# The last pair of down tiles of a mixture-of-experts layer: read as eight interleaved groups of sixteen rows in place of 128 adjacent rows

## The chip, the cores and the metric

One core of a Trainium2 chip runs the whole program. The metric is the device time of one execution in microseconds (us). The comparison is by the median of several executions; one execution was taken by the hardware profiler.

## What is computed

Two layers of a small network on 256 tokens of width 1024, in float32. The first has a recurrent mixer and a dense feed-forward block. The second has an mLSTM mixer and a mixture of eight experts, of which each token takes two. Only the end of the second matters here. Cut to that:

```python
def swiglu(x, w1, w3, w2):
    return (jax.nn.silu(x @ w1) * (x @ w3)) @ w2

def moe_swiglu(xn, w_router, w1, w3, w2):
    ...
    top_logit, top_idx = lax.top_k(logits, TOP_K)      # TOP_K = 2, N_EXPERTS = 8
    gates = jax.nn.softmax(top_logit, axis=-1)
    ...                                                # tokens gathered by expert
    yb = lax.map(expert_block, ...)                    # swiglu(xb, w1[e], w3[e], w2[e])
    ...
    out = jnp.zeros((T, D), xn.dtype).at[sorted_tok].add(y_slot)

x = x + moe_swiglu(rms_norm(x, norm_ffn), ...)
return rms_norm(x, final_norm)
```

w1 and w3 are [8, 1024, 2816], w2 is [8, 2816, 1024].

## The kernel before

The weights of the experts don't fit on the chip and pass through it once, in tiles of 128 partitions. The "up" weights (w1 and w3) come as 128 units of 1408 KB, from `moe13`, into ten slots. The "down" weights (w2) come as 88 pairs of 1024 KB, from `moe2`, into eight slots: `w2t`, four in the buffer W, three in S, and the eighth in x. A pair is 128 rows of 2048 float32, so 8 KB for each partition, and the 128 rows lie one behind the other in memory. There are NB = 11 pairs for each of E = 8 experts. Pair v is pair v mod 11 of the expert in place v // 11, and goes to slot v mod 8. Expert 7 in the order of places is the last; its pairs are v = 77 to 87. Pair 87, the last of all, goes to the slot in x.

All these transfers are issued by SyncE (SP) in one queue, in an order written out by hand: `first_refills` walks over the units and pairs in the order in which TensorE uses them. Before each it waits until TensorE has used the tile that stood in the same slot (`m_u` for units, `m_d` for pairs), and then issues the load of the tile that is ten units or eight pairs ahead. So pair 87 is issued when pair 79 is used. After it comes only the load of the weights of the final norm, `wrow`, 512 KB (4 KB for each partition, the same row for all). Which expert stands in which place is decided at run time; `chosen_rows` computes the address from a register.

Each load adds 16 to the semaphore of its slot. TensorE waits for it in `down` (the line before `w2p = ...`) and then runs 16 matmuls of 128x32 by 128x512 for the pair. In the last expert the pairs 0 to 10 run with nothing between them (`first_experts`), since all up units are done by then. Behind pair 87 come, in this order: ScalarE copies the result (L1644), TensorE scatters it to the tokens, VectorE adds it to the residual (L2325), ScalarE sums the squares (L1698), VectorE scales by the norm and by `wrow` (L2398), and SP writes the output (L649).

All matmuls of the kernel are recorded at one line, L692, the helper. The loads of pairs are L556, those of units L551, that of `wrow` L587.

Of the kernel before, what the change touches and what calls it, by code (L numbers as in the profile page):

```python
# [15 lines left out]
P = 128  # L16
T = 256
D = 1024
# [10 lines left out]
E = 8  # L29
# [9 lines left out]
NB = QN // 32  # L39
# [7 lines left out]
GATHERS = ((0, 1), (1, 4), (4, 8))  # L47
SMALL = (1, 4, 7)
SMALL_CAP = 64
ORDER = [7] + [SMALL.index(p) if p in SMALL else len(SMALL) + [q for q in range(1, E) if q not in SMALL].index(p) for p in range(1, E)]  # L50


# [20 lines left out]
def constants():  # L73

    s, t = np.arange(P)[:, None], np.arange(P)[None, :]
    c = np.zeros((P, NCONST), np.float32)
    c[:, IDENT:IDENT + P] = s == t
    c[:, BLK:BLK + P] = s // HD == t // HD
    c[:, ONES:ONES + P] = 1.0
    c[:, MEAN_D:MEAN_D + P] = 1.0 / D  # L80
    c[:, BLKM:BLKM + P] = (s // HD == t // HD) / HD
    c[:, SU:SU + P] = s < t
    c[:, FLOOR:FLOOR + P] = np.where(s <= t, 0.0, 1000.0)
    c[:, IOTA:IOTA + P] = t
    c[:, ROWS:ROWS + P] = np.concatenate([np.arange(32), np.arange(64, 96), np.arange(32, 64), np.arange(32, 64)])
    c[:, ROWS_LAST:ROWS_LAST + P] = np.concatenate([np.arange(32), np.arange(64, 96), np.arange(32), np.arange(64, 96)])
    c[:, RANKS:RANKS + E] = ORDER
    c[:, FIRST_KEY:FIRST_KEY + E] = [100000.0] + list(range(1, E))
    c[:, SHORT:SHORT + E] = [32.0 * (p in SMALL) for p in range(E)]
    c[:, CAPS:CAPS + E] = [SMALL_CAP if p in SMALL else SLOTS for p in range(E)]  # L90
    c[:, MEANS + 8] = 1.0 / D
    c[:, PICK:PICK + 32] = s % 32 == np.arange(32)[None, :]
    p = np.arange(P)
    c[:, TOK], c[:, TOK + 1] = p + 1, p + 1 + P
    c[:, QUARTER] = p // 32 - 4
    c[:, EVEN], c[:, ODD] = (p // 32) % 2 == 0, (p // 32) % 2 == 1
    c[:, EPS] = 1e-6
    c[:, EPS + 1] = 1e-5 * HD
    s, t = s % L, np.arange(L)[None, :]
    c[:, MASKS:MASKS + L] = s < t  # L100
    c[:, MASKS + L:MASKS + 2 * L] = s <= t
    c[:, EYE:EYE + L] = s == t
    low = np.zeros((P, LV, L), np.float32)
    for lv in range(LV):
        b = 1 << lv
        low[:, lv] = (s // (2 * b) == t // (2 * b)) & ((s // b) % 2 == 1) & ((t // b) % 2 == 0)
    c[:, LOW:LOW + (LV - 1) * L] = low[:, 1:].reshape(P, (LV - 1) * L)
    first = np.concatenate([(s // 2 == t // 2) & (s % 2 == 0) & (t % 2 == 1), low[:, 0] > 0], 1).astype(np.uint8)
    return c, first


def hybrid_rglru_rwkv7_mlstm_moe(nc, A, out):

    ctx = ExitStack()
    with ctx:
# [114 lines left out]
        u1, u2, u3 = [W[:, TMP + T * i:TMP + T * (i + 1)] for i in range(3)]  # L230
# [176 lines left out]
        def pair_slot(n, v):  # L407
            return v % (OVER_PAIRS if n else DSLOTS)
# [72 lines left out]
        def _(sp):  # L481
# [52 lines left out]
                sp.dma_start(m_all[:, h, :], m_rows[h:h + 1, :].broadcast_to([P, T])).then_inc(in_m, 16)  # L534
            u13 = A["moe13"].rearrange("(u p) n -> u p n", p=P)
            u2 = A["moe2"].rearrange("(u p) n -> u p n", p=P)

            expert = {}

# [4 lines left out]
            def chosen_rows(src, p, i, n):  # L544
                at = sp.snap(expert[p] * n + i, min_val=n, max_val=E * n - 1)
                return src[bass.ds(at, 1)].rearrange("u p n -> (u p) n")
# [5 lines left out]

            def load_d(n, v):
                p, i = divmod(v, NB)
                src = chosen_rows(u2, p, i, NB) if p else u2[v]
                sp.dma_start(w2t[pair_slot(n, v)], src).then_inc(in_d[pair_slot(n, v)], 16)  # L556

            def refill_unit(n, u):
# [9 lines left out]
            def refill_down(n, pair):  # L568
                ahead = OVER_PAIRS if n else DSLOTS
                if pair + ahead < PAIRED:  # L570
                    sp.wait_ge(m_d, PAIRED * n + pair + 1)
                    load_d(n, pair + ahead)

            def first_refills():
                for g in range(STAGES):
                    for k in range(KD):
                        refill_unit(0, g * KD + k)
                        if g * KD + k == KD + 2:
                            sp.wait_ge(ix_done, IX0 + 1)
                            load_d(0, 6)  # L580
                        for e, p in pairs_behind(g, k):
                            if NB * e + p + DSLOTS < NB * (E - 1):
                                refill_down(0, NB * e + p)
                for pair in range(NB * (E - 1) - DSLOTS, PAIRED - DSLOTS):
                    refill_down(0, pair)
                sp.wait_ge(m_u, LAST + 1)
                sp.dma_start(wrow, A["wf"].broadcast_to([P, D])).then_inc(in_wf, 16)  # L587
# [11 lines left out]

            load_u(0, 9)  # L600
            load_d(0, 3)
            sp.wait_ge(p1, 4)
            sp.dma_start(wo1, A["l1_w_out"].rearrange("(k p) n -> p k n", p=P)).then_inc(in_wo1, 16)
# [1818 lines left out]
def inputs_of(i):  # L2422

    def a(name):
        return np.asarray(i[name])
    o = {}
    o["xT"] = np.ascontiguousarray(a("x")[0].T)
    vecs = np.zeros((P, NV), np.float32)
    for name, at in VECS.items():
        if name == "moe_norm":  # L2430
            v = a("l1_norm_ffn").reshape(P, KD)
        else:
            v = a(name).reshape(-1, P).T
        vecs[:, at:at + v.shape[1]] = v
    o["vecs"] = vecs
    small = np.zeros((P, 4, 4, P), np.float32)
    for g, name in enumerate(("l0_gate_a_w", "l0_gate_x_w")):
        w = a(name).reshape(4, 2, HD, HD)
        for u in range(2):
            small[HD * u:HD * u + HD, g, :, HD * u:HD * u + HD] = w[:, u].transpose(1, 0, 2)  # L2440
    small[0:HD, 2] = a("l0_w_up").reshape(HD, 4, P)
    small[HD:, 2] = a("l0_a_up").reshape(HD, 4, P)
    small[:, 3] = a("l0_g_up").reshape(P, 4, P)
    o["small0"] = small.reshape(P, 2048)
    o["wqkv"] = np.ascontiguousarray(np.stack([a("l1_wq"), a("l1_wk"), a("l1_wv")]).transpose(2, 0, 1, 3)).reshape(P, 3 * D)
    wgt = np.zeros((P, KD, 40), np.float32)
    wgt[:, :, 0:8] = a("l1_w_in")[:, 2 * D + 8:].reshape(KD, P, 8).transpose(1, 0, 2)
    wgt[:, :, 32:40] = a("l1_w_in")[:, 2 * D:2 * D + 8].reshape(KD, P, 8).transpose(1, 0, 2)
    o["wgt"] = wgt.reshape(P, KD * 40)
    wrt = np.zeros((P, KD, 32), np.float32)  # L2450
    wrt[:, :, 0:E] = a("l1_router").reshape(KD, P, E).transpose(1, 0, 2)
    o["wrt"] = wrt.reshape(P, KD * 32)
    o["wf"] = a("final_norm").reshape(1, D)
    o["gb"] = np.ascontiguousarray(np.stack([a("l1_ig_b"), a("l1_fg_b")], 1))
    for name in ("l0_w_in", "l0_w_out", "l1_w_in", "l1_w_out"):
        o[name] = np.ascontiguousarray(a(name))
    w13 = np.stack([a("l0_ffn_w1"), a("l0_ffn_w3")]).reshape(2, KD, P, NPAIR, 2 * P)
    o["ffn13"] = np.ascontiguousarray(w13.transpose(3, 2, 0, 1, 4)).reshape(NPAIR * P, 2 * KD * 2 * P)
    o["ffn2"] = np.ascontiguousarray(a("l0_ffn_w2").reshape(NPAIR, 2, P, ND, 2 * P).transpose(3, 2, 1, 0, 4)).reshape(ND * P, 2 * NPAIR * 2 * P)

    def by_rows(w):
        rows = [w[e].reshape(KD, P, 4, 2, QN) if e < GATHERS[0][1] else w[e].reshape(P, KD, 4, 2, QN).transpose(1, 0, 2, 3, 4) for e in range(E)]
        return np.stack(rows).transpose(0, 4, 1, 2, 3, 5)

    w13 = np.stack([by_rows(a(name)) for name in ("l1_moe_w1", "l1_moe_w3")], 4)
    o["moe13"] = np.ascontiguousarray(w13).reshape(UNITS * P, 8 * QN)
    w2 = a("l1_moe_w2").reshape(E, 4, 2, NB, 32, D).transpose(0, 2, 3, 1, 4, 5)
    o["moe2"] = np.ascontiguousarray(w2.reshape(PAIRED, 2, P, D).transpose(0, 2, 1, 3)).reshape(PAIRED * P, 2 * D)
    o["cf"], o["lm"] = constants()
    return o  # L2470

# [12 lines left out]
```

## Time and profile before

| | us |
|---|---|
| median of 3 runs | 1156.12 |
| lowest and highest | 1155.8, 1158.51 |
| the profiled execution | 1159.16 |
| span of its profile, first to last instruction | 1156.7 |

| engine | busy us | share of the span |
|---|---|---|
| TensorE matmul (PE) | 1136.5 | 98% |
| TensorE weight load (PEld) | 726.2 | 63% |
| VectorE (DVE) | 420.5 | 36% |
| ScalarE (ACT) | 162.7 | 14% |
| GpSimd (POOL) | 34.7 | 3% |

The granted TensorE clock was 0.991 of full speed on average. In a view, "idle before <-releaser" tells how long the engine stood before the group and what ended it. The DMA share is the mean busy share of 16 DMA engines, so 0.50 can be eight engines busy and eight idle; a view names no DMA engine. In short windows it can come out a little over 1.

### The profile page before, as it was taken

How to read it: one execution, taken by the hardware profiler on the slowest of the kernel's cores; microseconds unless marked ns; L12 is line 12 of the kernel's file. 1: busy time of each engine (PE TensorE's matmuls, PEld its weight loads, DVE VectorE, ACT ScalarE, POOL GpSimd, SP SyncE). 2: the span in 40 equal slices, each digit the busy share in tenths (PEclk: the TensorE clock that was granted, in tenths of full speed). 3: DMA queues.
4: the chain of work that ended last, by engine and by line, in shares of the span. 5: the costliest groups of instructions: out<-in, count | busy, mean ns of one | idle time of the engine just before them, and what ended most of it. 6: DMA issues, size and time to landing. Idle time of an engine off the chain costs nothing.

```text
span 1156.7 us, 26746 instructions
## 1 busy us (share of the span) xinstructions
PE 1136.5 (98%) x12143; PEld 726.2 (63%) x12143; DVE 420.5 (36%) x926; ACT 162.7 (14%) x354; POOL 34.7 (3%) x34
## 2 busy tenths in 40 slices
PE   9999999999999999999999999999999999999995
PEld 7889879999999988874444344444444434444441
DVE  5756657787555375442221111210212022021011
ACT  4416212010000125323000000000000000000011
POOL 0013000000000000000110000100000000000000
PEclk9999889999999999999999999999999999999999
DMA  9800054445524528669999999999999999999994
GB/s 343 312 1 2 4 218 169 150 154 198 214 89 170 198 71 337 272 258 384 395 421 425 422 427 422 424 423 424 424 425 424 425 423 426 422 425 423 426 411 194
DMA packets 50104, 352.10 MB, mean 304 GB/s; under 512 B 4844, under 2 KB 10488, under 8 KB 20160
## 3 DMA queue, kind: packets, MB, share of 16 engines
q1 hardware_dynamic: 48384, 347.26, 73.5%
q0 software_dynamic: 1152, 2.90, 0.6%
q8 instruction: 97, 1.59, 0.5%
q10 hardware_dynamic: 448, 0.17, 0.1%
q14 instruction: 23, 0.19, 0.0%
HBM read 348.71 MB, written 2.11 MB: 303 GB/s over the span
## 4 chain that ended last, share of the span: by engine, by line
PE 95%; DMA 2%; DVE 2%; ACT 0%; issue 0%; DVEq 0%; SPq 0%
PE ps L692 94%; DMA x<-in_moe 1%; DMA W<-in_ffn 1%; PE ps L762 0%; DVE W L1875 0%; DVE xn L2398 0%; PE ps L1121 0%; ACT S L1698 0%; PE ps L1159 0%; DVE W L1963 0%; DVE W L1961 0%; DVE W L1901 0%; DVE S L1879 0%; ACT S L1463 0%; DVE W L1910 0%
## 5 line engine op out<-in xcount | busy, mean ns | idle before, releaser
L692 PE MATMUL ps<-W,S 128*32 128x352 f32 (+4 forms) x6216 | 490.7, 465 | 1.8 <-DMA W<-in_moe 0.8
L692 PEld LDWEIGHTS ps<-W,S 128*32 128x32 f32 (+2 forms) x6216 | 209.7, 112 | 270.7 <-issue 253.3
L692 PE MATMUL ps<-xn,W 128*128 128x256 f32 (+2 forms) x1232 | 223.1, 340 | 0.0
L692 PEld LDWEIGHTS ps<-xn,W 128*128 128x128 f32 (+1 forms) x1232 | 196.9, 191 | 23.2 <-issue 3.3
L692 PE MATMUL ps<-S,W 128*128 128x128 f32 (+3 forms) x1552 | 203.9, 293 | 1.4 <-DVE x L2052 0.7
L692 PEld LDWEIGHTS ps<-S,W 128*128 128x128 f32 (+2 forms) x1552 | 191.2, 192 | 9.1 <-issue 1.6
L2340 DVE TENSOR_TENSOR S<-S,ps 128x352 f32<-128x352 f32 x42 | 21.9, 521 | 420.1 <-ACT S L1636 417.4
L692 PE MATMUL ps<-S 128*32 128x512 f32 (+5 forms) x1502 | 125.3, 467 | 4.1 <-DMA S<-in_moe 2.7
L692 PEld LDWEIGHTS ps<-S 128*32 128x32 f32 (+2 forms) x1502 | 50.5, 115 | 72.9 <-issue 60.0
L1636 ACT ACTIVATE S<-ps 128x352 f32<-128x352 f32 x42 | 17.8, 462 | 544.9 <-PE ps L692 542.6
L692 PE MATMUL ps<-W 64*64 64x64 f32 (+2 forms) x1080 | 51.3, 238 | 2.6 <-DVE W L1901 1.6
L692 PEld LDWEIGHTS ps<-W 64*64 64x64 f32 (+2 forms) x1080 | 46.2, 146 | 5.1 <-DVE W L1901 2.2
L2302 DVE SCALAR_TENSOR_TENSOR xn<-ps,W,xn 128x512 f32<-128x512 f32 x28 | 19.7, 747 | 65.2 <-PE ps L692 65.2
L678 POOL DMA_INDIRECT S<-x_rows,gidx x18 | 18.3, 1018 | 349.0 <-DVE S L2313 312.7
L692 PE MATMUL ps<-x,S 128*32 128x512 f32 (+1 forms) x288 | 27.0, 510 | 0.5 <-DMA x<-in_moe 0.5
L2347 DVE STREAM_TRANSPOSE S<-S 128x352 f32<-128x352 f32 x42 | 22.9, 545 | 3.4 <-PE ps L1229 2.0
L692 PE MATMUL ps<-W,cf 64*128 64x512 f32 (+4 forms) x112 | 23.9, 506 | 0.0
L692 PEld LDWEIGHTS ps<-x,S 128*32 128x32 f32 x288 | 9.3, 110 | 17.3 <-issue 14.6
L692 PEld LDWEIGHTS ps<-W,cf 64*128 64x128 f32 (+1 forms) x112 | 10.4, 187 | 13.7 <-issue 13.2
L1541 ACT ACTIVATE W<-ps 128x128 f32<-128x128 f32 x10 | 2.8, 277 | 84.5 <-PE ps L692 84.5
L692 PE MATMUL ps<-S,cf 128*128 128x512 f32 (+2 forms) x38 | 12.5, 525 | 0.8 <-ACT S L1524 0.8
L1954 DVE TENSOR_TENSOR W<-W 128x1024 f32<-128x1024 f32 x10 | 12.3, 1225 | 0.3
(329 smaller groups left out, 560.1 us busy)
## 6 DMA issues: line engine op xcount, KB each, us to landing
W<-in_moe SPq DMA_DIRECT2D x116, 1408.0 KB, 30.1
W<-in_moe SPq DMA_DIRECT2D x44, 1024.0 KB, 30.5
S<-in_moe SPq DMA_DIRECT2D x33, 1024.0 KB, 29.8
W<-in_ffn SPq DMA_DIRECT2D x11, 2048.0 KB, 8.5
S<-in_moe SPq DMA_DIRECT2D x12, 1408.0 KB
W<-in_ffn SPq DMA_DIRECT2D x4, 2816.0 KB, 10.5
x<-in_moe SPq DMA_DIRECT2D x11, 1024.0 KB, 30.1
W<-in_l_w_in SPq DMA_DIRECT2D x4, 2048.0 KB, 20.3
```

Source lines behind the costliest of these rows:

```text
L678: nc.gpsimd.indirect_dma_start(landed[:, T * b:T * (b + 1)], None, x_rows.rearrange("r (i n) -> (r i) n", i=4), bass.IndirectOffsetOnAxis( ...
L692: return nc.tensor.matmul(o, l, r, start=start, stop=stop, **kw)
L1541: A_(silp[:, 0, :], ps[:, region(p, 0), TA], ACT.Silu)
L1636: A_(sil[:, i % 2, :], ps[:, 2 * t, 0:QN], ACT.Silu).then_inc(m_silu, 1)
L1954: step(V.tensor_tensor(t[:, 2], b21, t[:, 1], ALU.subtract), tw_done)
L2302: V.scalar_tensor_tensor(xtok[:, c, o], ps[:, 6 + i, :], rt[:, 8 + c, e:e + 1], xtok[:, c, o], ALU.mult, ALU.add).then_inc(m_add, 1)
L2340: V.tensor_tensor(hid, sil[:, i % 2, :], ps[:, 2 * t + 1, 0:QN], ALU.mult).then_inc(m_hid, 1)
L2347: V.transpose(hidT[:, h, t, :], hid).then_inc(m_ht, 1)
```

## The change

The host makes a second copy of one pair of each expert, pair 10, with its 128 rows in another order: row a·16 + b of the pair (a from 0 to 7, b from 0 to 15) stands at b·8 + a. In the first pass, the load of pair 10 of the last expert (pair 87) reads this copy as `a b n`: for each a the sixteen rows b, which lie eight rows apart. The same data arrives in the same partitions. The destination, its size, its slot, the wait before it, the place in the queue, the semaphore and the 8 KB runs are as before. The other 87 pairs are loaded as before.

```diff
+TURNED = (10,)
...
             u2 = A["moe2"].rearrange("(u p) n -> u p n", p=P)
+            u2_turned = A["moe2t"].rearrange("(u p) n -> u p n", p=P)
...
             def load_d(n, v):
                 p, i = divmod(v, NB)
-                src = chosen_rows(u2, p, i, NB) if p else u2[v]
+                if n == 0 and p == E - 1 and i in TURNED:
+                    src = chosen_rows(u2_turned, p, TURNED.index(i), len(TURNED)).rearrange("(b a) n -> a b n", a=8)
+                else:
+                    src = chosen_rows(u2, p, i, NB) if p else u2[v]
                 sp.dma_start(w2t[pair_slot(n, v)], src).then_inc(in_d[pair_slot(n, v)], 16)
...
     o["moe2"] = np.ascontiguousarray(w2.reshape(PAIRED, 2, P, D).transpose(0, 2, 1, 3)).reshape(PAIRED * P, 2 * D)
+    w2 = o["moe2"].reshape(E, NB, 8, 16, 2 * D)[:, list(TURNED)]
+    o["moe2t"] = np.ascontiguousarray(w2.transpose(0, 1, 3, 2, 4)).reshape(E * len(TURNED) * P, 2 * D)
```

## Rows read from the trace of the kernel before

**Rows 1.** Chain that ended last, from 540 us: start us, us, what.
```profile
548.58 578.49 PE ps L692 x7272
...
1127.24 16.91 DMA x<-in_moe
1144.14 0.04 issue
1144.19 1.97 PE ps L692 x16
1146.16 0.02 issue
1146.18 0.61 ACT W L1644
```

**Rows 2.** Timeline of the end, TensorE's matmuls: start us, us, what.
```profile
1126.85 3.62 PE L692 MATMUL ps<-W,S 128*32 128x512 f32 x32
...
1130.81 1.92 PE L692 MATMUL ps<-W,S 128*32 128x512 f32 x16 [0.34 <-DMA W<-in_moe]
...
1133.24 1.93 PE L692 MATMUL ps<-W,S 128*32 128x512 f32 x16 [0.51 <-DMA W<-in_moe]
...
1136.98 1.92 PE L692 MATMUL ps<-S 128*32 128x512 f32 x16 [1.81 <-DMA S<-in_moe]
...
1139.29 1.92 PE L692 MATMUL ps<-S 128*32 128x512 f32 x16 [0.39 <-DMA S<-in_moe]
...
1141.72 1.92 PE L692 MATMUL ps<-S 128*32 128x512 f32 x16 [0.51 <-DMA S<-in_moe]
...
1144.19 1.92 PE L692 MATMUL ps<-x,S 128*32 128x512 f32 x16 [0.55 <-DMA x<-in_moe]
```

**Rows 3.** Windows: length, PE, PEld, DVE, ACT, POOL busy, clock, DMA share, GB/s.
```profile
1080.00:1120.00 40.00, 40.00 (x504) 17.40 (x500) 4.96 (x8) 1.69 (x4) 0.00 (x0) 1.00 1.01 424
...
1134.00:1134.50 0.50, 0.50 (x8) 0.13 (x4) 0.00 (x0) 0.00 (x0) 0.00 (x0) 1.00 0.96 401
1135.00:1135.50 0.50, 0.16 (x4) 0.00 (x0) 0.00 (x0) 0.00 (x0) 0.00 (x0) 1.00 0.67 279
1136.00:1136.50 0.50, 0.00 (x0) 0.00 (x0) 0.00 (x0) 0.00 (x0) 0.00 (x0) 1.00 0.51 213
1138.00:1138.50 0.50, 0.50 (x12) 0.00 (x0) 0.00 (x0) 0.00 (x0) 0.00 (x0) 1.00 0.47 197
1140.00:1140.50 0.50, 0.50 (x8) 0.13 (x4) 0.00 (x0) 0.00 (x0) 0.00 (x0) 1.00 0.54 229
1142.00:1142.50 0.50, 0.50 (x8) 0.13 (x4) 0.00 (x0) 0.00 (x0) 0.00 (x0) 1.00 0.30 123
```

**Rows 4.** SP's own timeline at the end: start us, us, issue.
```profile
1127.24 0.33 SPq L556 DMA_DIRECT2D x<-in_moe  x1
1127.62 0.88 SPq L587 DMA_DIRECT2D W<-in_wf  x1
```

**Rows 5.** DMA issues between 1121 and 1129 us: size, median us to landing.
```profile
x<-in_moe SPq DMA_DIRECT2D x1, 1024.0 KB, 16.9
W<-in_wf SPq DMA_DIRECT2D x1, 512.0 KB, 17.8
```

**Rows 6.** DMA view, 423.4 to 424.9 us: a transfer of eight rows of 1 KB.
```profile
DMA packets 16, 0.01 MB, mean 5 GB/s; under 512 B 8, under 2 KB 16, under 8 KB 16
...
m_rows<-S SPq DMA_DIRECT2D x1, 8.0 KB
```

**Rows 7.** Timeline of the end: the first scaling by the final norm.
```profile
1151.21 0.75 DVE L2398 SCALAR_TENSOR_TENSOR xn<-xn,misc,W 128x512 f32<-128x512 f32 x1
```

**Rows 8.** The page, DMA queues: the fetches of instructions.
```profile
q8 instruction: 97, 1.59, 0.5%
```

## The prediction

> **What bounds the kernel now.** I read the chain that ended last first. From 548.58 us TensorE works for 578 us without a break, and then the chain leaves it once: for 16.91 us it runs through the load of pair 87, which is issued at 1127.24 and ends at 1144.14 [rows 1]. So the last stretch is set by loads, all before it by TensorE. The timeline of the end says how much that is. Pairs 80 and 81 run back to back, 3.62 us for both, 1.81 each. From pair 82 on there is a gap before every pair, each ended by the load of that pair: 0.34, 0.51, 1.81, 0.39, 0.51 and 0.55 us, in all 4.11 [rows 2]. These 4.11 us are all that any change of the last loads can win, and this change touches the load of pair 87 alone: directly it can take away the last gap, 0.55 us, and not the five before it.
>
> Then the windows, for the DMA engines. In the long stretch from 1080 to 1120 us they are full, at 424 GB/s; at that rate a pair of 1024 KB (1.05 MB) takes 2.47 us, and 2.43 and 2.47 us lie between the starts of pairs 85, 86 and 87 [rows 2, 3]. But from 1136 to 1141 us, while TensorE still waits for pairs, the share is only 0.51, 0.47, 0.54, at 197 to 229 GB/s [rows 3]. About eight of the sixteen engines have nothing left, and the other eight still carry the halves of pairs 84 to 87. Since each pair needs both halves, it lands when the late eight are done with it. In all, the early eight are idle from about 1136 until the landing at 1144.14, for 8 us.
>
> **What the change removes, adds and moves.** It moves nothing in order: the same wait, the same place in the queue, the same 1024 KB in 8 KB runs, no instruction more on TensorE. What it alters is the outermost dimension of the source: 8 in place of 128. The only transfer with eight outer rows that the trace shows by itself, m_rows, consists of 16 packets, eight with data and eight below 512 B, where one of sixteen shares would have 32 [rows 6]: it ran in eight shares. So I take it that pair 87 now runs in eight shares of sixteen rows, on eight engines with 128 KB each, while the other eight carry none of it. (The row allows another reading, that eight rows can't be cut into more; this is a rival below.)
>
> By the Trainium skill, "DMA: Bandwidth & Descriptors", section on why a DMA increments its semaphore by 16, the number of engines is the largest up to 16 that divides the slowest dimension of both sides. That would be 8 here, and on this queue the lowest-numbered eight; the row on m_rows agrees as far as the count goes, and no view shows the numbers.
>
> It then depends on whether those eight are the early or the late ones. I take the early ones. No view names an engine, so this is the weak point of the sum. What speaks for it: something loads the late eight more than the others over the long stretch, and the candidate is the fetching of instructions, 97 packets of 16 KB [rows 8]. The load of eight rows by ScalarE at the start of the program (`gb`), in the records of single packets behind the views, goes to eight engines of which none is the one that the first of these fetches delays. One fetch is thin evidence, hence the chance below.
>
> Forecast, the early eight carry it:
> - They had their own half of pair 87 and of `wrow` done by about 1136. Another 64 KB each is as much time as a whole pair at the full rate, 2.47 us, so pair 87 lands by about 1138.5. Even at half the rate for all its 128 KB, 9.9 us from about 1132.3 (1136 less 1.24 for `wrow` and 2.47 for the half pair), it would land at 1142.2.
> - The late eight reach pair 86 as before, since pair 87 stood behind it: TensorE starts pair 86 at 1141.72 [rows 2]. That pair takes 1.92 us, and pair 87 now follows with no gap, in 1.81 as pairs 80 and 81. It ends at 1145.45 where it ended at 1146.16 before [rows 1, 2].
> - Sum: 0.55 us of gap and about 0.1 of a matmul sequence that starts warm, -0.6 to -0.7 us. The next bound is pair 86 on the late eight, which the change leaves alone. ScalarE, scatter, norm and output follow pair 87 in a fixed chain and move with it.
>
> Costs that I put at nothing: SP's own issue, 0.33 us [rows 4], may grow with the extra dimension; a second added to it would still be hidden by the 5 us between 1138.5 and 1143.64. `wrow`, issued next, landed 17.8 us after 1127.62, at 1145.4, and is first used at 1151.21 [rows 4, 5, 7]; that cover of 5.8 us holds in every case below but the heaviest. Rows eight apart are still 8 KB runs, the form in which the kernel streams pairs now. I bound their price between nothing and half the rate, and take nothing.
>
> **The rivals.**
> *The eight are the late ones.* Each of them then carries 64 KB more in the stretch that TensorE waits for. The landing of pair 87 moves by a whole pair's time, 2.47 us, to 1146.6, and with it the end: +2.5 us, slower. This is the rival on the other side. It decides as soon as the eight chosen are behind the others by anything at all, and its price is paid in full since nothing hides pair 87. For it: by name alone it is as likely as the forecast. Against it: the packet records told above. If in addition the spaced rows ran at half the rate there, 9.9 us in place of 2.47 for the last pair, it would be +7.4 us; nothing in the rows points to that, and it is the only way past 0.3% that I can price.
>
> *The bytes still pass where the late eight write.* Sixteen rows of a share lie in sixteen partitions in place of eight, so early and late engines may write to the same part of the memory. If a late engine gave way for the half pair that goes to its partitions, it would lose what it was spared, up to 2.47 us, but now ahead of pair 86: that starts at 1144.19, pair 87 ends at 1147.9, +1.8 us. Half of that loss is +0.5. For it: the 424 GB/s in the full stretch are the same for units and pairs, so some limit common to all is at work, and the rows can't tell an engine's limit from a port's [rows 3]. Against it: the late eight would have to yield in full.
>
> The Trainium skill, "SBUF — State Buffer", section "Door 1: The DMA port swizzle", says that 64 adjacent partitions reach only eight of sixteen ports. By that rule the half of pair 87 for the late engines' partitions still goes through their ports, which is this rival; no row of the trace before has engines that share a port, so it shows neither.
>
> *It doesn't do what it says.* The transfer is still cut in sixteen (or SP's descriptors merge the dimensions again), and all times are those of before: 0.
>
> **How the numbers follow.** The profiled execution took 1159.16 us, 2.46 more than its span and 3.0 more than the median of the runs, 1156.12. The differences above are made on the span and I carry them over to the median unchanged, as the tail is the same work. The forecast is 1156.12 - 0.6 = 1155.5 us. The rivals: late eight 1158.6, in the heavy form 1163.5; shared ports 1156.6 to 1157.9; no effect 1156.1.
>
> Chances: early eight 0.60, late eight 0.17, late and heavy 0.03, shared ports 0.10, no effect 0.08, and 0.02 for something not foreseen that wins more. A measurement of this kernel can tell about 0.3% from no change, which is 3.5 us here, more than the forecast or any rival but the heavy one. So faster by over 0.3% gets 0.03 (the unforeseen, and a disturbed measurement), slower by over 0.3% 0.06 (the heavy form, and the late eight with a spread of the runs above the median, which reached 1158.51 before), within 0.3% 0.91. The range has the forecast with the spread of a median of the runs (the lowest was 0.3 below it) and reaches up to the late eight: 1154.4 to 1158.7.
>
> **What would show it right or wrong.** In the changed kernel's timeline the gaps before pairs 82 to 86 should stand as they are, and the gap before pair 87 be gone, with pairs 86 and 87 as one group of 32 matmuls. The load of pair 87 should land 11 us after its issue and not 16.9, and the chain should pass through pair 86's load. The DMA share should fall to a half later, about 1138.5 and not 1136, and the late eight run dry at about 1143 and not 1145.4. If the gap before pair 87 grows to about 3 us, the eight were the late ones. If pair 86 starts later than before, the ports are shared. If all rows are as before, the transfer wasn't cut in eight. The size of the forecast is wrong if the gaps of 82 to 86 change, since I say that nothing in them hangs on pair 87.

## The result: 0.63% slower

| | before | changed |
|---|---|---|
| median, us | 1156.12 | 1164.68 |
| lowest and highest of 5 runs, us | 1154.07, 1158.51 | 1161.0, 1165.29 |
| span of the profiled execution, us | 1156.7 | 1162.8 |

The ratio is 1.0063, with a 95% interval of 1.0051 to 1.0075, so about 7.3 us. (The two medians differ by 8.6 us and the two profiled spans by 6.1: a single execution of either kernel can lie some us off, and the account below, which is read from the two profiles, explains the 6.1.) The forecast was 1155.5 with a range up to 1158.7.

The chain of the changed kernel has the same shape as before [rows 1], with a load that takes longer: start us, us, what.

```profile
1127.72 22.57 DMA x<-in_moe2t
...
1150.33 1.97 PE ps L697 x16
```

The timeline of TensorE, the last expert's pairs. The first line holds pairs 80 to 82, each of the others one pair (the lines of the kernel moved by five, L692 is L697 now).

```profile
1127.33 5.53 PE L697 MATMUL ps<-W,S 128*32 128x512 f32 x48
...
1134.63 1.92 PE L697 MATMUL ps<-W,S 128*32 128x512 f32 x16 [1.77 <-DMA W<-in_moe]
...
1139.04 1.92 PE L697 MATMUL ps<-S 128*32 128x512 f32 x16 [2.49 <-DMA S<-in_moe]
...
1142.85 1.92 PE L697 MATMUL ps<-S 128*32 128x512 f32 x16 [1.89 <-DMA S<-in_moe]
...
1145.56 1.92 PE L697 MATMUL ps<-S 128*32 128x512 f32 x16 [0.79 <-DMA S<-in_moe]
...
1150.33 1.92 PE L697 MATMUL ps<-x,S 128*32 128x512 f32 x16 [2.85 <-DMA x<-in_moe2t]
```

The gaps add up to 9.79 us, against 4.11 before [rows 2]. Pair 86 starts 3.84 us later than before (1145.56 against 1141.72) and pair 87 6.14 us later (1150.33 against 1144.19). So the difference has two parts: 3.84 us in pairs that the change does not touch, and 2.30 us between pairs 86 and 87. Of the first part 0.48 us stood before the changed transfer was issued, at 1127.72 against 1127.24 [rows 4]; that much is a difference between the two executions, which leaves 3.36 us.

The windows say what happened to the first part. First two windows of the kernel before; the columns are those of [rows 3].

```profile
1131.00:1133.00 2.00, 1.73 (x16) 0.31 (x8) 0.00 (x0) 0.00 (x0) 0.00 (x0) 1.00 1.02 426
1133.00:1135.00 2.00, 1.76 (x16) 0.42 (x16) 0.00 (x0) 0.00 (x0) 0.00 (x0) 1.00 0.95 383
```

Then the changed kernel.

```profile
1129.00:1131.00 2.00, 2.00 (x24) 0.48 (x20) 0.00 (x0) 0.00 (x0) 0.00 (x0) 1.00 0.94 397
1131.00:1133.00 2.00, 1.86 (x16) 0.40 (x16) 0.00 (x0) 0.00 (x0) 0.00 (x0) 1.00 1.04 305
1133.00:1135.00 2.00, 0.37 (x4) 0.16 (x8) 0.00 (x0) 0.00 (x0) 0.00 (x0) 1.00 1.05 236
...
1146.00:1148.00 2.00, 1.48 (x16) 0.26 (x8) 0.00 (x0) 0.00 (x0) 0.00 (x0) 1.00 0.14 51
1148.00:1150.00 2.00, 0.00 (x0) 0.00 (x0) 0.00 (x0) 0.00 (x0) 0.00 (x0) 1.00 0.11 45
```

Read the last two columns together. At 1133 us all sixteen engines are busy (1.05), as before, but they move 236 GB/s and not 383. They are not short of work; each packet takes about twice as long. That includes the engines that are carrying pairs 83 to 86, whose loads are unchanged: in the records of single packets behind the views, none of the 8 KB packets that start from 1132 to 1141 us takes less than 0.38 us, and the median is 0.57; in the kernel before, from 1131 to 1133 us, it is 0.31. And at the very end, from 1146 to 1150 us, a share of 0.14 and 0.11 is about two engines of sixteen: TensorE waits for two stragglers. They are not slowed any more: 45 GB/s at a share of 0.11 is 26 GB/s for each engine that is busy, as in the full stretch (424 at 1.01), where the window from 1133 us gives 14.

The page shows that pair 87 did run in eight shares. Before, and changed:

```profile
q1 hardware_dynamic: 48384, 347.26, 73.5%
```

```profile
q1 hardware_dynamic: 48376, 347.26, 73.6%
```

Eight packets fewer with the same bytes: eight completion packets in place of sixteen.

### The profile page after: what moved, and what is told of

Its sections match the earlier page's. It is cut to its first block, busy times and chain, and to the rows that moved or that the text cites. A ratio compares the mean times of both kernels' runs of the same rounds, so it can differ in the third digit from the quotient of the medians.

```text
span 1162.8 us, 26746 instructions
## 1 busy us (share of the span) xinstructions
PE 1136.3 (98%) x12143; PEld 743.2 (64%) x12143; DVE 420.5 (36%) x926; ACT 162.7 (14%) x354; POOL 34.7 (3%) x34
## 4 chain that ended last, share of the span: by engine, by line
PE 94%; DMA 3%; DVE 2%; ACT 0%; issue 0%; DVEq 0%; SPq 0%
PE ps L697 94%; DMA x<-in_moe2t 2%; DMA W<-in_ffn 1%; PE ps L767 0%; DVE W L1880 0%; DVE xn L2403 0%; PE ps L1126 0%; PE ps L1164 0%; ACT S L1703 0%; DVE W L1968 0%; DVE W L1966 0%; DVE W L1906 0%; DVE S L1884 0%; ACT S L1468 0%; DVE W L1915 0%
## 5 line engine op out<-in xcount | busy, mean ns | idle before, releaser
L697 PE MATMUL ps<-W,S 128*32 128x352 f32 (+4 forms) x6216 | 494.1, 465 | 2.7 <-DMA W<-in_moe 1.8
L697 PEld LDWEIGHTS ps<-W,S 128*32 128x32 f32 (+2 forms) x6216 | 225.3, 112 | 258.0 <-issue 219.6
L697 PE MATMUL ps<-xn,W 128*128 128x256 f32 (+2 forms) x1232 | 222.4, 339 | 0.0
L697 PEld LDWEIGHTS ps<-xn,W 128*128 128x128 f32 (+1 forms) x1232 | 196.2, 190 | 23.2 <-issue 3.3
L697 PE MATMUL ps<-S,W 128*128 128x128 f32 (+3 forms) x1552 | 203.9, 292 | 1.9 <-DVE x L2057 0.8
L697 PEld LDWEIGHTS ps<-S,W 128*128 128x128 f32 (+2 forms) x1552 | 191.1, 192 | 9.6 <-issue 1.9
L697 PE MATMUL ps<-S 128*32 128x512 f32 (+5 forms) x1502 | 127.2, 466 | 6.6 <-DMA S<-in_moe 5.2
L697 PEld LDWEIGHTS ps<-S 128*32 128x32 f32 (+2 forms) x1502 | 53.1, 115 | 72.5 <-issue 53.5
L697 PE MATMUL ps<-W 64*64 64x64 f32 (+2 forms) x1080 | 51.8, 240 | 2.8 <-DVE W L1906 1.7
L697 PEld LDWEIGHTS ps<-W 64*64 64x64 f32 (+2 forms) x1080 | 46.5, 147 | 5.4 <-DVE W L1906 2.2
L697 PE MATMUL ps<-x,S 128*32 128x512 f32 (+1 forms) x288 | 27.6, 510 | 2.9 <-DMA x<-in_moe2t 2.9
L697 PE MATMUL ps<-W,cf 64*128 64x512 f32 (+4 forms) x112 | 23.9, 506 | 0.0
L697 PEld LDWEIGHTS ps<-x,S 128*32 128x32 f32 x288 | 10.1, 110 | 18.6 <-issue 12.7
L697 PEld LDWEIGHTS ps<-W,cf 64*128 64x128 f32 (+1 forms) x112 | 10.4, 186 | 13.7 <-issue 13.2
L697 PE MATMUL ps<-S,cf 128*128 128x512 f32 (+2 forms) x38 | 12.4, 524 | 0.8 <-ACT S L1529 0.8
L2330 DVE TENSOR_TENSOR xn<-xn,ps 128x512 f32<-128x512 f32 x4 | 2.6, 682 | 29.0 <-PE ps L697 29.0
```

The lines of the kernel that those rows point to most:

```text
L697: return nc.tensor.matmul(o, l, r, start=start, stop=stop, **kw)
L2330: return V.tensor_tensor(xtok[:, c, 512 * i:512 * (i + 1)], xtok[:, c, 512 * i:512 * (i + 1)], ps[:, 2 * c + i, :], ALU.add).then_inc(done, 1)
```

## The experiments

The first question was why packets slow down. Theory S: the rows of the source are spaced. Theory D: the shares of the destination crowd few places. The first four runs were to tell them apart. Unless said otherwise, each is an edit of the changed kernel, and only pair 87 is concerned.

**shares16**: interleaved, but in sixteen groups.

```diff
-  ... .rearrange("(b a) n -> a b n", a=8)
+  ... .rearrange("(b a) n -> a b n", a=16)
-    w2 = o["moe2"].reshape(E, NB, 8, 16, 2 * D)[:, list(TURNED)]
+    w2 = o["moe2"].reshape(E, NB, 16, 8, 2 * D)[:, list(TURNED)]
```

> The copy is turned for sixteen groups: the outermost dimension of the source is 16, each group is eight rows that lie sixteen apart, so the interleaved reading stays and the cut in eight shares is gone. Theory S (the spaced rows of the source are slow to read): pair 87 still lands late and the other pairs in flight slow down, so the gap before pair 87 stays above 1.5 us and the end is 3 to 7 us later than before. Theory D (eight shares of sixteen adjacent partitions crowd a few places of the on-chip memory): sixteen shares fill all of them, so the gaps are those of before (0.3 to 1.8 us, 4.1 in all) and the time is within 1.5 us of before.

**padded8**: eight groups, adjacent rows, one unused row behind each group of the copy.

```diff
-  ... .rearrange("(b a) n -> a b n", a=8)
+  ... .rearrange("(a b) n -> a b n", a=8)[:, 0:16, :]
```

> The copy keeps the sixteen rows of a group adjacent, and one unused row stands behind each group, so that the eight groups can't merge into 128 rows. Source rows adjacent, cut in eight shares as in the changed kernel. Theory S: no rows are spaced, so the slowing goes: pair 87 lands about 11 us after its issue, its gap is gone, and the end is 0.6 us earlier than before. Theory D: the destination is that of the changed kernel, so the result is too: gap before pair 87 near 2.9 us, gaps in all near 9.8 us, 5 to 8 us slower than before.

**low8** and **high8**: only half of the rows, in one transfer of eight groups of eight.

```diff
+  src = chosen_rows(u2_turned, p, ...)[0:64].rearrange("(b a) n -> a b n", a=8)      # high8: 64:128
+  sp.dma_start(w2t[pair_slot(n, v)][0:64, :], src).then_inc(in_d[pair_slot(n, v)], 16)
```

> Only rows 0 to 63 of pair 87 are loaded, to partitions 0 to 63, as eight groups of eight interleaved rows; rows 64 to 127 of that pair are left out, so half of its data isn't the pair's. Half the bytes: on eight engines 64 KB each, 2.5 us at full rate. Theory D in the form that the late engines are those that write partitions 64 to 127: nothing is in their way, so pairs 82 to 86 land as before and pair 87 follows with no gap: 0.6 us faster than before. Theory S: interleaved reading slows all engines while it lasts, for about half as long as in the changed kernel (some 5 us at half rate): pairs 84 to 86 land about 2 to 3 us later.

> The counterpart: only rows 64 to 127 of pair 87 are loaded, to partitions 64 to 127, in the same eight shares with the same bytes and the same spacing; rows 0 to 63 are left out. Theory D: the early engines now write where the late eight write, and the late eight lose up to the 2.5 us that these bytes take: pair 86 starts 1.5 to 2.5 us later than before, the end 1 to 2 us later. Theory S: the same time as with rows 0 to 63 alone, within 0.5 us.

| run | ratio to before | 95% interval |
|---|---|---|
| shares16 | 1.0056 | 1.0040 to 1.0073 |
| padded8 | 1.0058 | 1.0037 to 1.0079 |
| low8 | 1.0014 | 1.0003 to 1.0024 |
| high8 | 1.0040 | 1.0025 to 1.0055 |

The windows from 1133.5 to 1135.5 us of shares16 and from 1133 to 1135 us of padded8 and high8, and from 1129 to 1131 us of low8, which reached that point earlier:

```profile
1133.50:1135.50 2.00, 0.40 (x4) 0.16 (x8) 0.00 (x0) 0.00 (x0) 0.00 (x0) 1.00 0.92 193
```

```profile
1133.00:1135.00 2.00, 1.08 (x12) 0.29 (x12) 0.00 (x0) 0.00 (x0) 0.00 (x0) 1.00 1.00 223
```

```profile
1133.00:1135.00 2.00, 0.08 (x4) 0.09 (x8) 0.00 (x0) 0.00 (x0) 0.00 (x0) 1.00 1.03 207
```

```profile
1129.00:1131.00 2.00, 1.07 (x15) 0.16 (x8) 0.00 (x0) 0.00 (x0) 0.00 (x0) 1.00 1.06 233
```

All four run at 193 to 233 GB/s with a share of 0.92 to 1.06. padded8 has no spaced rows and is as slow, so S falls: the spacing isn't needed. But shares16 has sixteen shares, and D as I had written it fell with it; so did D's word on low8, where nothing should have slowed. high8 lost more than D said, 4.6 us against 1 to 2. What the four have in common is a source with two outer dimensions, and the copy. Three suspects were left. L: the copy lies in a slow place of memory. Form: any transfer with two outer dimensions slows the engines. P: with two outer dimensions a share is a run of adjacent partitions, whereas in a plain load of 128 rows each engine writes places that are its own.

What would an engine's own places be? The trace does not name them. By the Trainium skill, "DMA: Bandwidth & Descriptors", section "The descriptor swizzle", in a transfer to 128 partitions the first engine writes partitions 0 to 3 and 32 to 35, the second 4 to 7 and 36 to 39, and so on, eight engines for the partitions below 64 and eight for those above. The shares of P are an assumption about how such a transfer is cut; no row shows which partitions an engine writes. The two together suggested a test: a transfer of 32 partitions in eight groups of four rows keeps the first eight engines on their own places below partition 64, and puts them on the places of the other eight above it.

**copy16**: from the copy, in the order of the original, as 128 rows.

```diff
-  src = chosen_rows(u2_turned, p, TURNED.index(i), len(TURNED)).rearrange("(b a) n -> a b n", a=8)
+  src = chosen_rows(u2_turned, p, TURNED.index(i), len(TURNED))
```

> Pair 87 is read from a copy, but the copy has the order of the original and is read as 128 adjacent rows. All four experiments so far read from the copy and all were slow around pair 87, with or without spaced rows, so the copy's place in memory is suspected. Theory L (the place of the copy is slow to read): gap before pair 87 above 2 us, 5 us slower than before. Theory P (the shares of a source with two outer dimensions are adjacent partitions, so engines write across each other's places; read as 128 rows they don't): as before, gaps 4.1 us in all, within 1 us.

**orig8**: the changed access on the original.

```diff
-  src = chosen_rows(u2_turned, p, TURNED.index(i), len(TURNED)).rearrange("(b a) n -> a b n", a=8)
+  src = chosen_rows(u2, p, i, NB).rearrange("(b a) n -> a b n", a=8)
```

> Pair 87 is read from the original in eight interleaved groups, exactly as the changed kernel reads the copy; its rows therefore arrive in other partitions than they should, and the result of this pair is not the pair's. Theory L: the original is as fast as ever, so pair 87 lands early and the end is 0.6 us before that of before. Theory P: as in the changed kernel, gaps near 9.8 us in all, 5 to 8 us slower.

**quart_low**, **quart_all**, **quart_high**: two, four and two transfers of 32 partitions.

```diff
+  for q in (0, 1):                                            # all: (0, 1, 2, 3); high: (2, 3)
+      src = chosen_rows(u2_turned, p, ...)[32 * q:32 * q + 32].rearrange("(b a) n -> a b n", a=8)
+      sp.dma_start(w2t[...][32 * q:32 * q + 32, :], src).then_inc(in_d[...], 16)
```

> Only rows 0 to 63 of pair 87 are loaded (64 to 127 are left out), as two transfers of 32 partitions, each in eight interleaved groups of four rows. Same bytes on the same eight engines as the transfer of rows 0 to 63 in one piece, where packets slowed down to about half the rate; but each engine writes four adjacent partitions in each transfer and never shares a place with another. Theory P: no slowing; pair 87 lands by 1138.5 us, the share of the DMA engines stays at eight full engines, no longer gap before pairs 85 and 86 than before, 0.6 us faster than before. Theory L, or that any source with two outer dimensions slows the engines: slowed as the one-piece transfer was, 1 to 2 us slower than before.

> All of pair 87 as four transfers of 32 partitions in eight groups of four rows. Theory P: rows 0 to 63 are free of collisions, rows 64 to 127 are written by the early eight where the late eight write, one against one: the late eight lose up to 2.5 us. Between 0.5 us faster and 2 us slower than before, and in any case at least 3 us faster than the changed kernel. Theory L or slowing by form: as the changed kernel, 5 to 8 us slower.

> The mirror of the two transfers of rows 0 to 63: only rows 64 to 127 of pair 87 are loaded (0 to 63 are left out), as two transfers of 32 partitions in eight groups of four rows. Same form, bytes and engines; only the partitions differ. If an engine slows down when it writes places that another engine normally writes, and slows the others with it: while pair 87 is in flight all engines are busy at about half of 424 GB/s, and the end comes 2 to 4 us later than before (1.002 to 1.0035). If the slowing of the changed kernel came from the form of the transfer or the sixteen rows of a share: full rate and the time of before, as with rows 0 to 63.

**halves16**: no copy, no groups; the original as two transfers of 64 adjacent rows.

```diff
+  src = chosen_rows(u2, p, i, NB)
+  for h in (0, 64):
+      sp.dma_start(w2t[pair_slot(n, v)][h:h + 64, :], src[h:h + 64]).then_inc(...)
```

> No interleaving and no copy: pair 87 from the original as two transfers of 64 adjacent rows, each cut in sixteen shares of four rows by its 64 outer rows. All of the pair is loaded. If it is foreign places that slow the engines: half of the engines write foreign places in each transfer, and the engines run at about half rate while it lasts; 1 to 5 us slower than before (1.001 to 1.004). If the slowing needs a source with two outer dimensions: as before within 1 us.

| run | ratio to before | 95% interval |
|---|---|---|
| copy16 | 1.0004 | 0.9995 to 1.0014 |
| orig8 | 1.0074 | 1.0054 to 1.0095 |
| quart_low | 0.9998 | 0.9988 to 1.0009 |
| quart_high | 1.0028 | 1.0016 to 1.0041 |
| quart_all | 1.0035 | 1.0024 to 1.0045 |
| halves16 | 1.0057 | 1.0037 to 1.0077 |

The windows from 1131 to 1133 us of copy16 and orig8:

```profile
1131.00:1133.00 2.00, 1.92 (x16) 0.46 (x16) 0.00 (x0) 0.00 (x0) 0.00 (x0) 1.00 1.00 410
```

```profile
1131.00:1133.00 2.00, 0.69 (x8) 0.00 (x0) 0.00 (x0) 0.00 (x0) 0.00 (x0) 1.00 0.99 229
```

The copy is read at 410 GB/s, the original in eight groups at 229: L falls. Next quart_low, quart_high, quart_all and halves16:

```profile
1131.00:1133.00 2.00, 1.63 (x16) 0.29 (x12) 0.00 (x0) 0.00 (x0) 0.00 (x0) 1.00 1.03 416
...
1141.00:1143.00 2.00, 1.77 (x20) 0.58 (x24) 0.00 (x0) 0.00 (x0) 0.00 (x0) 1.00 0.12 47
```

```profile
1131.00:1133.00 2.00, 1.25 (x12) 0.16 (x4) 0.00 (x0) 0.00 (x0) 0.00 (x0) 1.00 1.01 244
1133.00:1135.00 2.00, 1.01 (x12) 0.42 (x16) 0.00 (x0) 0.00 (x0) 0.00 (x0) 1.00 0.98 211
```

```profile
1131.00:1133.00 2.00, 1.55 (x16) 0.29 (x12) 0.00 (x0) 0.00 (x0) 0.00 (x0) 1.00 0.95 379
1133.00:1135.00 2.00, 1.15 (x12) 0.13 (x4) 0.00 (x0) 0.00 (x0) 0.00 (x0) 1.00 1.01 244
```

```profile
1131.00:1133.00 2.00, 0.38 (x4) 0.00 (x0) 0.00 (x0) 0.00 (x0) 0.00 (x0) 1.00 1.10 248
```

quart_low and quart_high are the decisive pair. The form, the bytes and the two outer dimensions are equal; the partitions differ, and with them the rows of the copy that are read, but copy16 reads all 128 of these at 410. Partitions 0 to 63 are written at the full 416 GB/s, 64 to 127 at 244 and 211. low8 and quart_low are the second pair: the same rows go to the same partitions 0 to 63, and only the cut differs, shares of eight partitions or twice four. The first runs at 233 GB/s, the second at 416. quart_all runs through both: full first (379), then 244 when its upper half is on its way. halves16 slows too, with nothing but adjacent rows; its 6.6 us are more than the 1 to 5 that I expected, and in its profile 1.67 us of the loss are a lower clock at pair 87 (last section). So neither the spacing, nor the copy, nor the eight shares, nor the two dimensions are the cause. P fits all ten runs on pair 87 described so far: engines go at about half rate while the places an engine writes are not the ones it writes in a plain load of 128 rows. It needs one condition more, which the end of the changed kernel shows: by P its two stragglers write sixteen adjacent partitions each as well, but with the other engines idle they do so at 26 GB/s each, the full rate. So it takes other engines at work beside them; a foreign place alone costs nothing there. One expectation on quart_low failed: pair 87 was to land by 1138.5 us, and by the records of single landings it landed at 1141.8, its two late engines well after the other six (1135.3). My estimate for quart_all was too low, 2 us at most where 4.0 were measured: I had let only the late engines lose, and all of them do.

The section "Door 1: The DMA port swizzle" of "SBUF — State Buffer" in the Trainium skill gives a partition range of 64 only eight of the sixteen ports. The 248 GB/s of halves16 and 233 of low8 go with a half. But by that rule the engines that load pairs 83 to 86 through the other ports should keep their rate, and the share of about 1 with half the bytes says that they don't; on that the measurement decides.

**turn_mid**: does such a loss stay, if it falls where TensorE waits for no load? Pair 49 in place of pair 87.

```diff
-TURNED = (10,)
+TURNED = (5,)
-  if n == 0 and p == E - 1 and i in TURNED:
+  if n == 0 and p == 4 and i in TURNED:
```

> Pair 5 of the expert in place 4 (v = 49) is turned in place of pair 87, some 400 us before the end, where TensorE waits for no load. The slowed transfer costs the DMA engines about 5 to 6 us in a stretch in which they are full all the time. If such a loss can't be made up before the end, since the engines have no idle time there, it shows in full in the gaps before pairs 80 to 87: 4 to 7 us slower (1.0035 to 1.006). If the loads run far enough ahead to take it in, as TensorE never waits there: as before within 1 us.

The ratio is 1.0096 (1.0073 to 1.0119), 11 us: more than I expected of the losing side, and more than the same transfer costs at the end. Its windows:

```profile
860.00:870.00 10.00, 10.00 (x112) 4.51 (x107) 2.82 (x4) 0.12 (x1) 0.00 (x0) 1.00 1.02 417
870.00:880.00 10.00, 10.00 (x128) 3.96 (x124) 0.00 (x0) 0.00 (x0) 0.00 (x0) 1.00 1.01 223
880.00:890.00 10.00, 10.00 (x124) 3.77 (x116) 1.88 (x4) 0.82 (x2) 0.00 (x0) 1.00 1.00 231
890.00:900.00 10.00, 7.11 (x72) 3.19 (x68) 3.27 (x10) 0.00 (x0) 1.99 (x2) 0.83 1.01 422
```

For 20 us all engines run at about 227 in place of 424 GB/s: 20 · (1 - 227/424) = 9.3 us of transfer lost, from one transfer of 1 MB. It lasts so long because it holds as long as any of the eight shares is on its way, and the shares are not in step. By the records of single landings six have landed by 882.6 us and two land at 890.4, and in between, with two shares left in flight, nothing recovers:

```profile
884.00:890.00 6.00, 6.00 (x76) 2.29 (x72) 1.88 (x4) 0.82 (x2) 0.00 (x0) 1.00 0.98 226
```

I had expected the loss to show in the gaps before pairs 80 to 87. It shows earlier: those gaps are 4.24 us in all, as before, and TensorE loses its clear run at 890 us.

```profile
893.72 10.71 PE L697 MATMUL ps<-W,S 128*32 128x352 f32 x112 [2.90 <-DVE S L2318]
906.02 9.32 PE L697 MATMUL ps<-W,S 128*32 128x352 f32 x116 [1.59 <-DMA W<-in_moe]
```

The view puts the first wait down to VectorE, but that instruction had ended by 893.11, and the unit issued at 851.88 landed at 893.62: this too is a wait for a load. The two profiled spans differ by 7.0 us. Since the engines are full from there to the end (423 GB/s from 1080 to 1120 us), nothing is made up. (The turned pair came some 310 us before the end, not 400.)

**own128**: the second part by itself, 128 KB on each of the eight engines at full rate. The quart_low transfers twice, once to the slot and once to an idle slot of an up unit.

```diff
+  sp.wait_ge(m_u, UNITS)
+  for to in (w2t[pair_slot(n, v)], slots[(LAST + 2) % USLOTS][:, 0:2 * D]):
+      for q in (0, 1):
+          ...
+          sp.dma_start(to[32 * q:32 * q + 32, :], src).then_inc(in_d[...], 16)
```

> Measures the second term by itself. Rows 0 to 63 of pair 87 are loaded twice, each time as two transfers of 32 partitions in eight groups of four rows, once to their slot and once to a slot of an up unit that is no longer used; TensorE waits for both. Rows 64 to 127 are left out. The same eight engines carry 128 KB each, as in the changed kernel, but no engine writes another's place. Theory now: the cost of the change has two terms, (1) all engines at about half rate while foreign places are written, 3.8 us by the start of pair 86, and (2) two of the eight engines belong to the late set and carry 64 KB more at the very end, 2.3 us. Here only (2) is left: the rate stays full, pairs 82 to 86 start as before, the gap before pair 87 grows from 0.55 to about 3 us while about two engines are busy (share 0.12), and the end is 2 to 2.6 us later than before (1.0017 to 1.0023). Rival: all eight engines of such a transfer are early, and the late landing in the changed kernel came from the slowing alone: then no gap before pair 87, and the time of before.

The ratio is 1.0008 (0.9998 to 1.0019), about 0.9 us where I expected 2 to 2.6. A window during the load, one at its end, and TensorE's last pair:

```profile
1131.00:1133.00 2.00, 1.65 (x16) 0.31 (x8) 0.00 (x0) 0.00 (x0) 0.00 (x0) 1.00 0.99 385
...
1143.00:1145.00 2.00, 1.41 (x16) 0.29 (x12) 0.00 (x0) 0.00 (x0) 0.00 (x0) 1.00 0.11 45
```

```profile
1144.30 1.92 PE L704 MATMUL ps<-x,S 128*32 128x512 f32 x16 [0.59 <-DMA W<-in_moe2t]
```

Half of the expectation holds: the rate is full, and at the end about two engines are at work (0.11), so two of the eight are late ones, which refutes the rival. The price does not hold. The records of single landings say why. The late eight are spread over 2.6 us: in own128 they finish pair 86 between 1139.1 and 1141.8 us. The two that carry pair 87 land it at 1144.0 and 1144.3, which is about 1139.1 and 1139.3 plus 128 KB at full rate, 4.9 us. They were among the first of the late, and the slowest of the late eight would have landed its own 64 KB at 1144.2 anyway. In the changed kernel the late eight finish pair 86 between 1143.8 and 1145.5, the two stragglers land pair 87 at 1148.9 and 1150.3, and the last of them was near the end of its set. So the second part was nothing in own128's profile and 2.30 us in that of the changed kernel; by this account it depends on how far back the two stand among the late. That account rests on two profiles.

None of these runs beat the kernel before. quart_low, which leaves half of the last pair out, closes the last gap and is still within noise of before (0.9998). What a steering of the last load can win, the last gap of 0.55 us, is less than these runs can tell from nothing. Pair 87 of quart_low, with no wait before it:

```profile
1142.97 1.90 PE L702 MATMUL ps<-x,S 128*32 128x512 f32 x16
```

## Why the prediction was wrong, point by point

- **What bounds the kernel**: right. The last stretch hangs on loads, and what lies behind pair 87 moved with it one for one.
- **The transfer is cut in eight shares**: right, from [rows 6] and the packets of the page.
- **"Rows eight apart are still 8 KB runs ... and take nothing"**: the price of the source was rightly put at nothing (quart_low reads spaced rows at 416 GB/s, and padded8 is slow without any). But the sum had no term for the destination, and this is the step that failed. It should have held a second question beside how many engines: which partitions each now writes. I had it only as the rival of shared places, and there bounded it by what one half pair takes, 2.47 us, on the late engines alone. It measured 3.84 us by the start of pair 86, 3.36 without what stood before, since all sixteen went to half rate, for about ten us. That bound came from the bytes of pair 87; the real price comes from the bytes of everyone for the time that pair 87 is on its way.
- **"I take the early ones"**: wrong, and not in a way that I had listed. The eight are six early and two late engines. In the changed kernel six shares landed between 1141.0 and 1143.8 us and two at 1148.9 and 1150.3. The thought that the engines form two halves, one of which the transfer takes as a whole, was an assumption that [rows 3] don't give: a share of 0.5 counts engines and doesn't say which. The argument from the first instruction fetch was too thin. Cost in the changed kernel: 2.30 us; I had priced the late rival at 2.47, and its sign, a gap of about 3 us before pair 87, came (2.85).
- **"The gaps before pairs 82 to 86 should stand as they are"**: wrong for 83 to 86, and this was the sign I had named that the size fails. "If pair 86 starts later than before, the ports are shared" pointed the right way.
- **The heavy form, +7.4 us**, has the measured size (+7.3), but by another sum: not the last pair at half rate on the late eight, but all pairs in flight at half rate, and two stragglers after it. That the sizes agree is luck. A chance of 0.03 was far too low, given that nothing in the rows bounded the destination.
- **Cover**: SP's issue took 0.80 us where a plain one takes 0.33 [rows 4], and no row shows it to cost anything, as forecast.
- **The range**: its lower end, 1154.4, doesn't follow from the words on it; 1155.5 less 0.3 is 1155.2. The measurement lies beyond the upper end, so nothing hangs on it.

## What to carry to other kernels

When a transfer's outer dimension is changed, ask not only on how many DMA engines it runs but which partitions each engine then writes; here a transfer of 1 MB with the wrong partitions about halved the rate of all sixteen engines for 10 to 20 us. Idle DMA engines beside a late transfer are no free capacity if the late bytes belong to partitions that only the busy engines write at full rate. And where the engines are full to the end, loads that run far ahead need not hide a loss in the middle: turn_mid, the one run on this, cost 11 us, though at its place TensorE waited for no load in the kernel before.

## What the runs showed of the hardware that I had not expected

- The slowing is not confined to the engines that leave their places: in low8 and quart_high eight engines carry the transfer, and all sixteen are busy at half the rate. In quart_high the partitions 64 to 127 take the bytes of both sets at once, so a limit of these places could be enough. It isn't for low8, which writes only below 64, nor for turn_mid, where two shares in flight hold all sixteen at 226 GB/s. How it spreads is open; no run here separates it.
- In some runs the TensorE clock fell after waits for loads. shares16: after a wait of 2.08 us in a window in which it was busy for 0.40 of 2 us, the granted clock was 0.55 in the next window and the sixteen matmuls of a pair took 3.10 us in place of 1.92. In halves16 pair 87, after a wait of 2.81 us, ran at 0.56 of full speed, near the lower of the two levels (1.2 of 2.4 GHz), and took 3.59 us; shares16 has the same at its pair 87 (3.56 us). So some 1.6 us of what these two profiles lose is clock, at the last pair alone. In the profile of the changed kernel, with waits of 2.49 and 2.85 us, it didn't fall, so it is no part of the 6.1 us.

```profile
1135.11 3.10 PE L697 MATMUL ps<-W,S 128*32 128x512 f32 x16 [2.08 <-DMA W<-in_moe]
```

```profile
1135.50:1137.50 2.00, 2.00 (x16) 0.35 (x8) 0.00 (x0) 0.00 (x0) 0.00 (x0) 0.55 1.03 240
```
